# Strassen's seven products for a quarter of ten feed-forward input chunk pairs, with two of four weight differences on GpSimd

## What is computed

```python
h = rms_norm(x, ffn_pre_gain[l])
gt, up = jnp.split(h @ w_ffn_in[l], 2, axis=-1)      # w_ffn_in: 2048 x 11264
x = x + rms_norm((jax.nn.silu(gt) * up) @ w_ffn_out[l], ffn_post_gain[l])
```

## Time and profile before

| | us |
|---|---|
| median of 3 runs | 1517.09 (1516.76 to 1517.3) |
| the profiled execution | 1516.52 |
| its span in the trace | 1514.6 |
| PE busy | 1505.1 (99%) |
| PE weight loads busy | 1239.9 (82%) |
| DVE busy | 959.1 (63%) |
| ACT busy | 815.5 (54%) |
| POOL busy | 151.4 (10%) |
| granted TensorE clock, share of full | 0.999 |

### The profile page before, as it was taken

The page is one execution under the profiler, slowest core; times in us unless marked ns, Lnnn a source line. Parts: engine busy times, 40 slices in busy tenths (PEclk is TensorE's granted clock), DMA queues, the critical chain, the costliest instruction groups (busy, mean ns, idle before and its releaser), DMA issues.

```text
span 1514.6 us, 20541 instructions
## 1 busy us (share of the span) xinstructions
PE 1505.1 (99%) x6814; PEld 1239.9 (82%) x6814; DVE 959.1 (63%) x1283; ACT 815.5 (54%) x1102; POOL 151.4 (10%) x286
## 2 busy tenths in 40 slices
PE   9999999999999999999999999999999999999997
PEld 7887887888888888888888888888888888888886
DVE  7878988754644677557585566666555665444444
ACT  7645445666566444656566555555555554444342
POOL 0000000231120000000000222220122222000000
PEclk9999999999999999999999999999999999999999
DMA  9755555666555656855454666665666666655553
GB/s 342 235 184 179 178 183 183 197 201 191 183 187 179 235 185 218 294 197 203 156 187 157 209 208 200 210 203 197 204 206 208 206 208 221 209 195 195 195 193 126
DMA packets 89837, 304.80 MB, mean 201 GB/s; under 512 B 13056, under 2 KB 13568, under 8 KB 88768
## 3 DMA queue, kind: packets, MB, share of 16 engines
q1 hardware_dynamic: 80144, 285.12, 57.0%
q0 software_dynamic: 9216, 18.63, 3.7%
q10 hardware_dynamic: 432, 0.45, 0.1%
HBM read 294.19 MB, written 2.10 MB: 196 GB/s over the span
## 4 chain that ended last, share of the span: by engine, by line
PE 98%; DVE 1%; ACT 0%; DMA 0%; issue 0%; DVEq 0%; POOL 0%; SPq 0%; ACTq 0%; POOLq 0%
PE acc L1506 17%; PE acc L1508 17%; PE acc L1507 17%; PE side L1506 11%; PE side L1508 11%; PE side L1507 11%; PE tr L1508 3%; PE tr L1506 3%; PE tr L1507 3%; PE tr L1523 1%; PE acc L1744 1%; PE acc L1742 1%; PE acc L1743 1%; PE side L1529 0%; PE side L1564 0%; DMA raw<-in_units 0%
## 5 line engine op out<-in xcount | busy, mean ns | idle before, releaser
L872 DVE TENSOR_TENSOR w_lo<-raw,w_hi 128x1024 fp32r<-128x1024 f32 x350 | 428.6, 1226 | 322.1 <-ACT w_hi L453 317.7
L453 ACT ACTIVATE w_hi<-raw 128x1024 fp32r<-128x1024 f32 x350 | 370.3, 1060 | 416.3 <-PE acc L1508 232.1
L880 DVE SCALAR_TENSOR_TENSOR w_lo<-raw,cols,w_hi 128x512 fp32r<-128x512 f32 x352 | 248.7, 748 | 184.1 <-ACT w_hi L461 182.9
L461 ACT ACTIVATE w_hi<-raw,cols 128x512 fp32r<-128x512 f32 x352 | 234.9, 716 | 196.9 <-PE side L1508 98.0
L1506 PE MATMUL acc<-w_hi,xT_hi 128*128 128x512 f32 x824 | 322.8, 392 | 0.0
L1508 PE MATMUL acc<-w_hi,xT_lo 128*128 128x512 f32 x824 | 320.8, 389 | 0.0
L1507 PE MATMUL acc<-w_lo,xT_hi 128*128 128x512 f32 x824 | 320.8, 389 | 0.0
L1506 PE MATMUL side<-w_hi,xT_hi 128*128 128x512 f32 x480 | 187.1, 390 | 0.0
L1507 PE MATMUL side<-w_lo,xT_hi 128*128 128x512 f32 x480 | 186.8, 389 | 0.0
L1508 PE MATMUL side<-w_hi,xT_lo 128*128 128x512 f32 x480 | 186.8, 389 | 0.0
L1506 PEld LDWEIGHTS acc<-w_hi,xT_hi 128*128 128x128 f32 x824 | 154.7, 188 | 34.3 <-issue 1.9
(11 more groups left out here) (371 smaller groups left out, 1786.4 us busy)
## 6 DMA issues: line engine op xcount, KB each, us to landing
raw<-in_units SPq DMA_DIRECT2D x530, 512.0 KB, 3.4
hT_st<-h_blk POOLq DMA_DIRECT2D x176, 32.0 KB, 2.9
x_tok<-in_x SPq DMA_DIRECT2D x4, 512.0 KB, 5.8
qkT<-qk_blk POOLq DMA_DIRECT2D x64, 32.0 KB, 2.8
xres<-in_x POOLq DMA_DIRECT2D x1, 2048.0 KB, 10.5
m_raw<-in_mem_t POOLq DMA_DIRECT2D x1, 2048.0 KB, 8.6
mq<-in_mem POOLq DMA_DIRECT2D x1, 2048.0 KB, 15.4
x_raw<-in_x_t SPq DMA_DIRECT2D x6, 256.0 KB, 6.2
```

Of the source, the lines that this page charges most:

```text
L453: a_.activation(w_hi[:, j % RING], raw[:, j % RING], ACT.Copy).then_inc(hi_ready, 1)
L461: last = a_.activation(dst[:, j % RING, k], raw[:, j % RING, k], ACT.Copy, scale=cols[:, c:c + 1])
L872: v_.tensor_tensor(w_lo[:, s], raw[:, s], w_hi[:, s].bitcast(F32), ALU.subtract).then_inc(lo_ready, 1)
L880: last = v_.scalar_tensor_tensor(lo[:, s, k], raw[:, s, k], cols[:, c:c + 1], hi[:, s, k].bitcast(F32), ALU.mult, ALU.subtract)
```

## The change

For pairs 1 to 10, the first quarter of the 2048 input rows (four blocks of 128; two units of the gate chunk and two of the up chunk) is computed by Strassen's scheme in its form with seven products. Token half 0 and 1 and the even and odd row blocks are the 2x2 of the left matrix; row parity and gate or up are the 2x2 of the right one, W11 (gate, even), W12 (up, even), W22 (up, odd), W21 (gate, odd), each 256 rows by 512 columns and loaded as one unit.

- **Weights.** The seven right factors are W11, T1 = W12 - W11, T2 = W22 - W12, T3 = W22 - T1, W22, W21 and T4 = W21 - T3, in this order. T1, T3 and T4 overwrite W11 in `raw`, T2 overwrites W12. POOL makes T1 and T2 (`weight_differences`), DVE makes T3 and T4 (`difference` in its `split_in`). A pair now has 19 splits in place of 16: seven factors, then 12 plain units.
- **PE.** Each product (`pair_product`) is six matmuls, for one token half or sum of halves. Products 1 to 4 go to `side[2]`, `side[3]`, `tr[0]` and `tr[1]` (the first is used in all sums, so it has a bank of its own). Products 5, 6 and 7 start the banks of up half 0, gate half 0 and gate half 1, which the plain units go on with; up half 1 starts with a plain unit. Then come 12 plain units of 12 matmuls, six of the gate chunk and six of the up chunk.
- **Sums.** ACT copies product 1 into SBUF; DVE adds it and products 2 to 4 up in four instructions of 128x512 (`u_part`, `u_done`), adds them to the gate bank halves (`gate_sum`) and to the up bank halves (`up_sum`), and multiplies (`hidden_product`). SiLU now reads SBUF.
- **Left factors.** `ffn_pre_gain` moves from the weights to the activations: DVE scales each turned quarter into `xg` (`x2_scale`), from which `xT_hi` and `xT_lo` are made. DVE makes four sums of blocks of `xg` once (`S_f`, 128x256 each, in pair 0), and ACT and DVE split them.
- **Splits.** All units of the stage are split with one 128x1024 instruction on ACT and one on DVE.
- **Loads and loops.** SP waits for other counts (`load_late`): the slots of the four factors come free after factors 3, 5, 6 and 7. The ten pairs are unrolled on all engines. The host's order of the units changes to match.

The diff, cut to its core:

```diff
+S_FI, S_FO, S_END = 284, 474, 562
+def pair_base(i):
+    return S_FI + FI_SPLITS * (i - 1)
...
+def pair_slot(i, k):
+    return (k + i - 1) % RING
...
+            def load_late(u, slot, splits):
+                sp_.wait_ge(lo_ready, splits)
+                sp_.dma_start(raw[:, slot].rearrange("p a b -> p (a b)"), units[u]).then_inc(w_landed[slot], 16)
+            for i in range(1, 11):
+                u, v = U_FI + FI_LOADS * i, pair_base(i)
+                for k in range(4):
+                    load_late(u + k, pair_slot(i, k), v - 3 + k)
+                for d in range(12):
+                    load_late(u + 4 + d, plain_slot(i, d), v + (3, 5, 6, 7)[d] if d < 4 else v + d + 4)
...
+            def weight_differences(i):
+                turn = 16 * ((U_FI + FI_LOADS * i) // RING + 1)
+                b11, b12, b22, _ = (pair_slot(i, k) for k in range(4))
+                pool.wait_ge(lo_ready, pair_base(i) + 1)
+                pool.wait_ge(w_landed[b12], turn)
+                g.tensor_tensor(raw[:, b11], raw[:, b12], raw[:, b11], ALU.subtract).then_inc(t_ready, 1)
+                pool.wait_ge(w_landed[b22], turn)
+                pool.wait_ge(t_ready, 4 * i - 3)
+                g.tensor_tensor(raw[:, b12], raw[:, b22], raw[:, b12], ALU.subtract).then_inc(t_ready, 1)
+            for i in range(1, 11):
+                weight_differences(i)
+                spread_blocks(i)
+            spread_blocks(11)
...
+                v, turn = pair_base(i) + j, (U_FI + FI_LOADS * i) // RING + 1
+                if j >= W_SPLITS:
+                    d = j - W_SPLITS
+                    split_at(plain_slot(i, d), turn + 1 + d // RING, v)
+                elif j in (0, 4, 5):
+                    split_at(pair_slot(i, {0: 0, 4: 2, 5: 3}[j]), turn, v)
+                else:
+                    act.wait_ge(t_ready, 4 * i - 4 + {1: 1, 2: 2, 3: 3, 6: 4}[j])
+                    act.wait_ge(unit_used, v - (RING - 1))
+                    a_.activation(w_hi[:, v % RING], raw[:, pair_slot(i, 1 if j == 2 else 0)], ACT.Copy).then_inc(hi_ready, 1)
...
+                    if j == 8:
+                        act.wait_ge(unit_used, pair_base(i) + 1)
+                        if i == 1:
+                            act.wait_ge(acc_taken[1], G_FI + 2)
+                        else:
+                            act.wait_ge(hb_ready, i - 1)
+                        a_.activation(silu_g[:, 0], side[:, 2], ACT.Copy).then_inc(p1_copied, 1)
+                    if j == 13:
+                        hidden_hi(i)
+                        for h in range(HALVES):
+                            act.wait_ge(acc_taken[h], i * 2 + (G_FI + 1))
+                            a_.activation(silu_g[:, h], silu_g[:, h], ACT.Silu, scale=r_of(N_X2, h)).then_inc(silu_ready, 1)
+                    split_in(i, j + RING)
...
+                b11, b12, b22, b21 = (pair_slot(i, k) for k in range(4))
+                def difference(n, dst, minuend, subtrahend):
+                    dve.wait_ge(t_ready, 4 * i - 5 + n)
+                    v_.tensor_tensor(raw[:, dst], raw[:, minuend], raw[:, subtrahend], ALU.subtract).then_inc(t_ready, 1)
+                if j == 2:
+                    dve.wait_ge(lo_ready, pair_base(i) + 2)
+                    difference(3, b11, b22, b11)
+                if j == 4:
+                    dve.wait_ge(lo_ready, pair_base(i) + 4)
+                    dve.wait_ge(w_landed[b21], turn)
+                    difference(4, b11, b21, b11)
+                slot = plain_slot(i, j - W_SPLITS) if j >= W_SPLITS else (b11, b11, b12, b11, b22, b21, b11)[j]
+                split_at(slot, pair_base(i) + j)
...
+            def x2_scale(h, n):
+                dve.wait_ge(x2_turned, 4 * h + n + 1)
+                gains = cols[:, C_FFN + 4 * n:C_FFN + 4 * n + 4].unsqueeze(2).to_broadcast([P, 4, P])
+                v_.tensor_tensor(xg[:, h, n], tr[:, n % 2].rearrange("p (k t) -> p k t", k=4), gains, ALU.mult).then_inc(x2_scaled, 1)
...
+            def up_sum(i, h):
+                if h == 0:
+                    dve.wait_ge(acc0_full, i * 2 + G_FI + 2)
+                else:
+                    dve.wait_ge(unit_used, pair_base(i + 1))
+                    dve.wait_ge(u_done, i)
+                v_.tensor_tensor(hb[:, h], bank(1, h), hb[:, h], ALU.add).then_inc(acc_taken[h], 1)
...
+                    if j == 4 and i > 1:
+                        up_sum(i - 1, 1)
+                    if j == 5 and i > 1:
+                        hidden_product(i - 1)
+                    if j == 6:
+                        hidden_turn(i)
+                    if j == 9:
+                        dve.wait_ge(unit_used, pair_base(i) + 4)
+                        dve.wait_ge(h_blocked, i)
+                        dve.wait_ge(p1_copied, i)
+                        v_.tensor_tensor(hb[:, 0], tr[:, 1], silu_g[:, 0], ALU.add).then_inc(u_part, 1)
+                    if j == 10:
+                        dve.wait_ge(u_part, 3 * i - 2)
+                        v_.tensor_tensor(silu_g[:, 1], tr[:, 0], hb[:, 0], ALU.add).then_inc(u_part, 1)
+                        dve.wait_ge(u_part, 3 * i - 1)
+                        v_.tensor_tensor(hb[:, 0], side[:, 3], hb[:, 0], ALU.add).then_inc(u_part, 1)
+                    if j == 11:
+                        dve.wait_ge(u_part, 3 * i)
+                        v_.tensor_tensor(hb[:, 1], side[:, 3], silu_g[:, 1], ALU.add).then_inc(u_done, 1)
+                    if j == 12:
+                        gate_sum(i, 0)
+                        gate_sum(i, 1)
+                    if j == 14:
+                        hidden_lo(i)
+                    if j == 18:
+                        up_sum(i, 0)
+                    split_in(i, j + RING)
...
+            def pair_product(v, dst, hi, lo, begin, end):
+                pe.wait_ge(lo_ready, v + 1)
+                whi, wlo = w_hi[:, v % RING], w_lo[:, v % RING]
+                for q in range(2):
+                    pe.matmul(dst, hi(q), whi[:, q], start=(begin and q == 0), stop=False)
+                    pe.matmul(dst, hi(q), wlo[:, q], start=False, stop=False)
+                    mm = pe.matmul(dst, lo(q), whi[:, q], start=False, stop=(end and q == 1))
+                mm.then_inc(unit_used, 1)
...
+            pe.wait_ge(s_lo, 1)
+            for i in range(1, 11):
+                v = pair_base(i)
+                if i > 1:
+                    pe.wait_ge(u_done, i - 1)
+                pair_product(v, side[:, 2], *x_block(0, 0), True, True)
+                pair_product(v + 1, side[:, 3], *x_sum(0), True, True)
+                pair_product(v + 2, tr[:, 0], *x_sum(2), True, True)
+                pair_product(v + 3, tr[:, 1], *x_sum(1), True, True)
+                pe.wait_ge(acc_taken[0], i * 2 + G_FI)
+                pair_product(v + 4, side[:, 0], *x_sum(3), True, False)
+                pair_product(v + 5, acc[:, 0], *x_block(1, 0), True, False)
+                pe.wait_ge(acc_taken[1], i * 2 + (G_FI - 1))
+                pair_product(v + 6, acc[:, 1], *x_block(1, 1), True, False)
+                plain_units(v + W_SPLITS, 0, 4, None)
+                plain_units(v + W_SPLITS + 6, 1, 4, i * 2 + G_FI)
...
+            order += [blocks[0][0], blocks[1][0], blocks[1][1], blocks[0][1], pair[0][2:], pair[1][2:]]
```

More of the change, by code:

```diff
@@ L906, in hidden_turn @@
             def hidden_turn(i):
-                for h in range(HALVES):
-                    dve.wait_ge(acc_taken[h], i * 2 + G_FI)
+                if i == 1:
+                    for h in range(HALVES):
+                        dve.wait_ge(acc_taken[h], i * 2 + G_FI)
+                else:
+                    dve.wait_ge(hb_ready, i - 1)
                 for h in range(HALVES):
@@ L1424, in _, with x_sums @@
+            x2_update(1, 3)
             x2_lo_part(1, 1)
-            x2_update(1, 3)
-            gained_split(U_FI + 8, 8)
+            split_first(8)
+            x2_scale(1, 2)
             x2_lo_part(1, 2)
-            gained_split(U_FI + 9, 9)
+            split_first(9)
+            x2_scale(1, 3)
             x2_lo_part(1, 3)
-            gained_split(U_FI + 10, 10)
-            gained_split(U_FI + 11, 11)
+            split_first(10)
+            split_first(11)
             inverse(N_X2, D, 34)
-            def product_half(i):
+            def x_sums():
+                a = [[xg[:, h, 0].rearrange("p (q e) t -> p e q t", e=2)[:, e] for e in range(2)] for h in range(HALVES)]
+                own.link(v_.tensor_tensor(S_f[:, 0], a[1][0], a[1][1], ALU.add))
+                own.link(v_.tensor_tensor(S_f[:, 1], S_f[:, 0], a[0][0], ALU.subtract))
+                v_.tensor_tensor(S_f[:, 2], a[0][0], a[1][0], ALU.subtract)
+                v_.tensor_tensor(S_f[:, 3], a[0][1], S_f[:, 1], ALU.subtract).then_inc(s_ready, 1)
@@ L1466, in _ @@
+            for i in range(1, 11):
+                ffn_in(i)
             for n in range(4):
                 for j in range(22 * n, 22 * n + 22):
+                    if j == 0:
```

(41 more changed lines are left out.)

224 lines of the change are left out of this document (128 added, 96 removed).

## The result

The changed kernel takes **1531.79 us** (median of 4 runs, 1531.6 to 1533.25) beside 1517.19 for the kernel before (4 runs on the same chip): ratio 1.0097, 95% interval 1.0081 to 1.0113. It is 14.6 us slower. The forecast was slower by 4.1 us, so the direction held and the size did not. The time lies inside the forecast range of 1507 to 1532 us by 0.2 us only, and that end was worked out for a slower POOL (G = 2.8), which is not what happened; that the range held is luck.

A forecast was written before the change was run, and what follows sets the result against it. PE, busy 99% of the span, was taken as the bound: -13.6 (fewer matmuls) + 15.2 (stalls) + 1.8 (way in) + 0.7 (pair 1) = +4.1 us, forecast 1521.2 us, range 1507 to 1532.

The forecast's parts named there:

- a slower POOL: Rival: POOL's differences take 2.6 us or more each; at 2.90 the time is 1534 us; chance 0.16.
- G: Time of one weight difference (T1 or T2) on POOL, taken as 2.24 us from a whole copy scaled by four.
- The way in: Start of the feed-forward stage: DVE's scales delay the first low part and PE, +1.8 us, with 0 and 3 as ends.
- The chain through the factors: Splits and differences of factors 1 to 5 on ACT, DVE and POOL, timed from PE's possible start of product 1.
- 2G + 2.27: Predicted end in us of DVE's low part of factor 5, counted from PE's possible start of product 1.
- the formula: PE's stall per pair at factors 3 to 5: 2G - 2.96 us, forecast as 1.5 us.
- the 1.11 us behind T2: DVE's low part of factor 2 meets T2 on POOL and ends 1.11 us after it, at 2G - 4.34.
- The rival of cheap differences: POOL's differences are cheap or don't hold DVE up; 1506.0 us at G = 1.12, 1510 with overlap; chance 0.29.
- late loads: Rival: weight units land 2 us later than the median, PE waits another microsecond a pair; 1531 us; chance 0.07.
- 15.2 + 1.8 + 0.7: Forecast added PE waits in us: stall in ten pairs, the start of the feed-forward stage, and pair 1's two products.
- The four sums and their split in pair 0 lie under plain units.: In pair 0, making and splitting the sums of input blocks was taken as covered by PE's plain units, no cost.
- I cost the 12 plain units and the sums beside them at nothing: In each pair's plain units, DVE was given 2.72 us for 1.13 us of split and at most two short instructions.

The follow-up runs named there:

- writes: Changed kernel with T2 on POOL replaced by memsets of about the same length that read nothing; 1524.07 us.
- the longer turn: Changed kernel with one more unused 128x512 difference on POOL ahead of T1 in each pair; 1544.22 us.
- the later tile: Changed kernel with ACT's high part and DVE's low part of the transposed hidden tile each one step later; 1526.33 us.

## Why the prediction was right and wrong

**Right, by its own steps.** The 60 matmuls go, and PE's pace of 0.2265 us holds. The way in was put at +1.8 us, and PE stands there 4.19 - 2.35 = 1.84 us longer; in four of the runs above that leave this place alone (T2 on DVE, writes, the longer turn, the later tile) it stands for 3.5 to 4.0 us, so part of this close agreement is chance. The chain through the factors was right in order, in its start and in its end: in pair 3, counted from PE's product 1, the low part of factor 1 ends at -5.58 us (forecast -5.64) and that of factor 5 at 7.03 (7.05 by 2G + 2.27 with the measured G). Three pairs without other trouble wait 1.78 to 1.79 us, the formula gives 1.82. That two engines that read hold each other up was read from the earlier trace rows, as was the 1.11 us behind T2; the measured 1.08, and the undisturbed 1.23 beside writes, bear it out. The rival of cheap differences was wrong with it, and so was that of late loads, although its sign came: ACT's list has 70.5 us of waits on raw, where before it had 1.1 in this stage. The sign did not tell the two apart, since these waits do not reach PE. The rival of a slower POOL, which began at G = 2.6, gave 1534 us; the time came near it, but G did not, and most of what was missing came from elsewhere.

**Wrong, by the size of terms.** The shortfall is 30.3 us of standing against 20.0 forecast (2.35 that was there, and 15.2 + 1.8 + 0.7 by the sum), and has three parts.
- *G was 2.24 and is 2.39.* It enters twice a pair, 0.3 us, or **3 us** in ten pairs. Scaling the whole of a copy by four was nearer than its slope (1.9) or the low bound (1.12), and still low by 6%.
- *"The four sums and their split in pair 0 lie under plain units."* They do not. S_lo stands between the low parts just ahead of factor 1, which then ends at -3.6 and not at -5.64. Pair 1 waits 4.44 us where 1.82 + 0.7 was to be had: **1.9 us**, and the run with the sums two steps earlier takes just this away.
- *"I cost the 12 plain units and the sums beside them at nothing".* This counted the busy time of DVE and ACT in a unit, but not a wait of ACT. In the new order of a pair (19 steps in place of 16, the transposes at step 6 in place of 1), spreading the hidden tile and splitting it came from 11 steps apart to 7, its DMAs land later as well, and ACT waits 20.4 us in ten times for it. The splits behind it reach the factor chain late: over 1.79 us a pair, pairs 2, 5, 6, 7, 9 and 10 stand for **5.5 us** more. The run with the split a step later takes 4.3 of them away; 1.2 in pair 10 remain, where a wait of 2.4 us for the tile is left. The prediction looked at POOL's 16 DMAs only as to whether they hold POOL's differences up, not at who waits for their landing. This is the step that should have been made: for each moved consumer, how far it is now from its producer, in us. With the landings of the kernel before, that distance would still have looked just wide enough for most pairs; it would have shown a margin of 1.3 us or less where there had been 13 to 15.

3 + 1.9 + 5.5 = 10.4, beside the 10.3 us by which the sum of the waits was short. By the medians the forecast was short by 10.6 us.

**Pair 10** is the longest because of its tile wait, 4.66 us on ACT; PE then stood for 2.17 us at one matmul:

```profile
1225.24 1.06 ACT L585 ACTIVATE hT_hi<-hT_st 128x1024 fp32r<-128x1024 f32 x1 [4.66 <-DMA hT_st<-h_blk]
...
1239.26 0.50 PE L1985 MATMUL side<-w_hi,S_hi 128*128 128x512 f32 x1 [2.17 <-DVE w_lo L963]
...
1242.25 0.63 PE L1986 MATMUL tr<-w_lo,S_hi 128*128 128x512 f32 x1
1242.68 0.63 PE L1987 MATMUL tr<-w_hi,S_lo 128*128 128x512 f32 x1
...
1245.88 0.47 PE L1985 MATMUL side<-w_hi,S_hi 128*128 128x512 f32 x1 [0.18 <-DVE w_lo L963]
```

Behind the wait the granted clock fell. By windows of 2 us (us, PE's busy time and count, clock, DMA share, GB/s):

```profile
1240.00:1242.00 2.00, 1.56 (x5) 0.61 0.00 0
1242.00:1244.00 2.00, 2.00 (x6) 0.54 0.64 193
1244.00:1246.00 2.00, 1.82 (x9) 1.00 0.17 70
```

The two matmuls at 1242.25 and 1242.68 are 0.43 us apart, near the 1.2 GHz level, in place of 0.2265. Five distances are stretched, by about 1.1 us in all, and yet this cost nothing: at 1245.88 PE waits again for DVE, for the low part of factor 5, which comes when DVE's own chain delivers it, 6.53 us behind the low part of factor 2 (6.51 in pair 3). The slow matmuls filled time in which PE would have stood anyway. In the other nine pairs the clock did not fall. How long one wait is does not decide it alone: in the run with the longer turn of POOL one of 2.23 us in pair 1 left the clock at 1.00, and one of 3.60 us in pair 10 did not. That run's waits and the windows behind them (these with all five engines):

```profile
837.75 0.50 PE L1987 MATMUL side<-w_hi,S_hi 128*128 128x512 f32 x1 [2.23 <-DVE w_lo L965]
...
1253.48 0.57 PE L1987 MATMUL side<-w_hi,S_hi 128*128 128x512 f32 x1 [3.60 <-DVE w_lo L965]
```
```profile
838.00:840.00 2.00, 1.41 (x6) 0.80 (x5) 2.00 (x2) 1.01 (x2) 0.00 (x0) 1.00 0.00 0
...
1254.00:1256.00 2.00, 2.00 (x7) 1.30 (x5) 2.00 (x3) 1.27 (x2) 0.00 (x0) 0.50 0.00 0
```

**Which pairs pay for the tile.** A pair's tile wait delays the factors of the next pair. Ahead of pairs 3, 4 and 8 ACT waits for 0.92, 1.39 and 0.75 us, the three shortest of the waits ahead of pairs 2 to 10, and these pairs show no cost; ahead of the others it waits for 1.78 us or more, and they do. The longest, ahead of pair 10, has a reason of its own: `h_blk` is done at 1208.06 and POOL's first DMA of that tile starts only 3.40 us later, at 1211.46, in place of 0.29. The change did not bring this: in the kernel before, the same tile has the same 3.40 us (1187.29 to 1190.69), where nothing waited for it.

**What stays open.** Why the small DMAs land later than before (a median of 4.9 us in place of 2.9) was not tried; the loads of units land later too, 4.1 in place of 3.4. Nothing in the trace releases POOL at the end of the 3.40 us. Of the span's growth 1.0 us is outside the places above.
